# Group norm roots by token on 12 columns, spread back by a matmul, in the SSD mixer of a two-layer decoder step

## The reference, cut to what matters

```python
y = (y_diag + y_off) ...            # the scan over 4 chunks of 128 tokens, 4 heads a group
y = y + xs * d_skip[:, None]
y = y.reshape(b, l, D_INNER) * jax.nn.silu(z)
yg = y.astype(jnp.float32).reshape(b, l, SSD_GROUPS, D_INNER // SSD_GROUPS)
yg = yg * lax.rsqrt(jnp.mean(yg * yg, axis=-1, keepdims=True) + RMS_EPS)
y = (yg.reshape(b, l, D_INNER) * norm_g).astype(h.dtype)
return y @ w_out, new_conv, new_ssm
```

## Time and profile before

| what | value |
|---|---|
| median of 3 runs | 1629.84 us (1626.79 to 1630.45) |
| the profiled execution, its own time | 1631.33 us |
| the profiled execution, its span from first to last instruction | 1629.6 us |
| mean granted TensorE clock | 0.975 |
| busy: PE, DVE, ACT, POOL | 1523.5, 1179.9, 686.1, 596.4 us |
| the mixer's windows | from about 76 to 567 us of the span |

### The profile page before, as it was taken

One profiled execution on the slowest core, in us unless ns is written; L12 is line 12 of the kernel. 1 busy time (PEld: TensorE's weight loads), 2 busy tenths in 40 slices (PEclk: granted clock), 3 DMA queues, 4 the chain that ended last, 5 costly groups with the idle time before them and its releaser, 6 DMA issues.

```text
span 1629.6 us, 30561 instructions
## 1 busy us (share of the span) xinstructions
PE 1523.5 (93%) x12329; PEld 1501.4 (92%) x12329; DVE 1179.9 (72%) x1533; ACT 686.1 (42%) x1043; POOL 596.4 (37%) x573
## 2 busy tenths in 40 slices
PE   5898987989888799999999999999999999999996
PEld 5888877979888789999999999999999999999996
DVE  4678898883888788979798453464454897979943
ACT  4746645623566243434343333342233343434321
POOL 3076676650776732314156122200002141404801
PEclk9998998999999899999999999999999999999998
DMA  6444445443434332332323332223222323242311
GB/s 165 112 137 141 133 137 152 138 134 117 144 121 134 113 105 78 104 104 79 110 98 104 96 113 78 84 74 94 89 78 78 104 79 104 79 130 79 128 55 53
DMA packets 158931, 173.44 MB, mean 106 GB/s; under 512 B 13912, under 2 KB 146896, under 8 KB 158784
## 3 DMA queue, kind: packets, MB, share of 16 engines
q1 hardware_dynamic: 137032, 131.30, 25.6%
q0 software_dynamic: 9472, 26.50, 5.1%
q10 hardware_dynamic: 12288, 13.71, 3.0%
HBM read 159.53 MB, written 12.21 MB: 105 GB/s over the span
## 4 chain that ended last, share of the span: by engine, by line
PE 62%; DVE 1%; issue 1%; ACT 1%; POOL 0%; ACTq 0%; DVEq 0%
PE ps L941 28%; PE ps L662 17%; PE ps L966 15%; PE ps L1048 1%; PE ps L682 1%; DVE rstd L1806 0%; PE ps L1016 0%; DVE w_lo L2111 0%; PE ps L919 0%; PE ps L705 0%; PE ps L770 0%; POOL ssum L1595 0%; ACT arena L1539 0%; ACT w_hi L1434 0%; PE ps L1088 0%
## 5 line engine op out<-in xcount | busy, mean ns | idle before, releaser
L662 PE MATMUL ps<-h_hi,w_hi 128*128 128x260 f32 (+2 forms) x1296 | 276.8, 296 | 9.3 <-issue 4.7
L662 PE MATMUL ps<-h_lo,w_hi 128*128 128x260 f32 (+2 forms) x1296 | 266.8, 288 | 0.0
L662 PE MATMUL ps<-h_hi,w_lo 128*128 128x260 f32 (+2 forms) x1296 | 266.6, 288 | 0.0
L1434 ACT ACTIVATE w_hi<-w 128x512 fp32r<-128x512 f32 x232 | 138.2, 626 | 241.6 <-PE ps L941 161.6
L662 PEld LDWEIGHTS ps<-h_hi,w_hi 128*128 128x128 f32 x1296 | 208.4, 195 | 11.4 <-issue 9.2
L941 PE MATMUL ps<-h_hi,w_hi 128*128 128x260 f32 x1024 | 206.6, 283 | 4.7 <-DVE work L2143 4.5
L2111 DVE TENSOR_TENSOR w_lo<-w,w_hi 128x512 fp32r<-128x512 f32 x232 | 189.6, 844 | 25.1 <-ACT w_hi L1434 24.6
L662 PEld LDWEIGHTS ps<-h_lo,w_hi 128*128 128x128 f32 x1296 | 207.0, 195 | 0.0
L941 PE MATMUL ps<-h_hi,w_lo 128*128 128x260 f32 x1024 | 206.4, 283 | 0.0
L662 PEld LDWEIGHTS ps<-h_hi,w_lo 128*128 128x128 f32 x1296 | 206.4, 194 | 0.0
L941 PE MATMUL ps<-h_lo,w_hi 128*128 128x260 f32 x1024 | 206.0, 283 | 0.0
(11 more groups left out here) (259 smaller groups left out, 3617.3 us busy)
## 6 DMA issues: line engine op xcount, KB each, us to landing
w<-in_mlp_w_up SPq DMA_DIRECT2D x32, 1024.0 KB, 5.4
w<-in_mlp_w_down SPq DMA_DIRECT2D x32, 1024.0 KB, 5.1
w<-in_ssd_w_in SPq DMA_DIRECT2D x16, 1024.0 KB, 6.7
w<-in_cm_w_in SPq DMA_DIRECT2D x16, 1024.0 KB, 5.4
w<-in_ssd_w_in SPq DMA_DIRECT2D x16, 512.0 KB, 5.7
arena<-in_state_ssm POOLq DMA_DIRECT2D x64, 128.0 KB, 3.4
arena<-scr_a ACTq DMA_DIRECT2D x16, 512.0 KB, 3.6
arena<-scr_bc POOLq DMA_DIRECT2D x32, 256.0 KB, 3.7
```

What stands on the lines that cost most here:

```text
L662: mm = pe.matmul(ps[:, 2 * slot + b, 0:tn], w[:, pair.w_slot, k, col:col + P], x[:, k, t0:t0 + tn], start=(k == 0 and n == 0), stop=(k == ...
L1434: nc.scalar.activation(blocks(w_hi)[:, (p.ring + n) % 8], src, ACT.Copy)\
```

## The change

POOL's `y_sum` is gone. PE sums the squares of both tiles itself, into bank 6: for each of the four chunks two matmuls with one column of ones leave the sums token by token on the partitions (4 columns), and two more leave the 8 samples' sums on all partitions (8 columns). ACT takes the root of these 12 columns into `r_y`, and DVE their reciprocal (`y_recip`). ACT then scales the 128x128 identity by each of the 4 columns (`y_diagonal`, into `sq`), PE multiplies that with ones (`spread`), which puts the 512 reciprocals on every partition of bank 7, and `y_norm` reads them there. It has four instructions in place of two.

The same change moves work in the windows. DVE takes `decayed(g, 1)` ahead of `decayed(g, 0)`. `y_norm` stands behind the next weight split and `evac_unit(nxt, 0)`, `y_diag(g, 0)` behind `evac_unit(nxt, 1)`, the `xdte` product ahead of the second weight split and of `conv(nxt, 1)`, and `conv(nxt, 2)` behind `states(g)`. PE's `spread` stands behind `gu(nxt, 0)`, its waits for `comb_done` ahead of `state_out` and the B and C transposes become waits for `combine`'s first instruction, and `raw_tr(nxt, 1)` goes behind `gu(nxt, 2)`. After window 7 `spread(7)` stands between `gu(8, 6)` and `gu(8, 7)`.

```diff
--- before.py
+++ after.py
@@ -268,6 +268,7 @@
         ssm_stage = carve(2, N)
         xdts = carve(2, NS)
         ysmp = carve(2, NS)
+        r_y = carve(NC + NS)
         at[0] = dt_at
         dt_v = carve(T, parts=HEADS)
...
@@ -741,7 +743,7 @@
                     pe.wait_ge(crow_done, 2)
                     pe.wait_ge(convf_ready, 2)
                     if due(g - 1):
-                        pe.wait_ge(yroot_done, g - 1)
+                        pe.wait_ge(ynorm_done, 2 * (g - 1))
                 pe.transpose(ps[0:35, 7, t * P:(t + 1) * P], raw[:, t % 2, TP:TP + 35], ident[:, :])\
                   .then_inc(cst_tr, 1)
@@ -763,20 +765,32 @@
                 if g < 0:
                     return
-                pe.wait_ge(ysum_done, g + 1)
+                pe.wait_ge(ysq_done, 2 * g + 2)
+                pe.wait_ge(comb_done, 2 * g + 2)
+                parts = (ssum[:, :], sq[:, 0, :])
+                for c in range(NC):
+                    for i, part in enumerate(parts):
+                        pe.matmul(ps[:, 6, c:c + 1], part[:, c * CH:(c + 1) * CH], ones[:, 0:1], start=(i == 0), stop=(i == 1))
+                for i, part in enumerate(parts):
+                    mm = pe.matmul(ps[:, 6, NC:NC + NS], ones[:, 0:1].to_broadcast([P, P]), part[:, TP:T],
+                                   start=(i == 0), stop=(i == 1))
+                mm.then_inc(rms_done, 1)
+
+            def spread(g):
+
+                if g < 0:
+                    return
                 pe.wait_ge(cst_evac, min(g + 2, GROUPS))
-                pe.wait_ge(comb_done, 2 * g + 2)
-                for b in range(2):
-                    mm = pe.matmul(ps[:, 6 + b, 0:TH], ones[:, 0:1].to_broadcast([P, P]),
-                                   ssum[:, b * TH:(b + 1) * TH], start=True, stop=True)
-                mm.then_inc(rms_done, 1)
+                pe.wait_ge(diag_done, g + 1)
+                pe.matmul(ps[:, 7, :], ones[:, 0:1].to_broadcast([P, P]), sq[:, 0, 0:TP], start=True, stop=True)\
+                  .then_inc(spread_done, 1)
             def state_out(g):
                 if g < 0:
                     return
                 pe.wait_ge(hstep_done, 4 * g + 4)
-                pe.wait_ge(comb_done, 2 * g + 1)
+                pe.wait_ge(cchain, 6 * g + 1)
                 for i in range(2):
                     mm = pe.transpose(ps[:, 5, 256 + i * N:256 + (i + 1) * N], hprev[:, 3, i * P:(i + 1) * P], ident[:, :])
                 mm.then_inc(h4_tr, 1)
@@ -796,8 +810,8 @@
                                    A[:, 1, c * CH:(c + 1) * CH], start=True, stop=True)
                 mm.then_inc(cb_done, 1)
-                if due(2 * g - 1):
-                    pe.wait_ge(comb_done, 2 * g - 1)
+                if due(g):
+                    pe.wait_ge(cchain, 6 * (g - 1) + 1)
                 state_out(g - 1)
                 for i in range(2):
                     mm = pe.transpose(ps[0:NS, 5, i * N:(i + 1) * N], A[:, i, S0:CONV_N:TAPS], ident[:, :])
@@ -818,11 +832,12 @@
                 rms(g - 1)
                 if nxt < GROUPS:
                     gu(nxt, 0)
+                    spread(g - 1)
                 for i in range(2):
                     pe.wait_ge(xdt_done, 2 * g + i + 1)
                     for hh in range(2):
-                        pe.wait_ge(m_done, 4 * g + 2 * i + hh + 1)
+                        pe.wait_ge(m_done, 4 * g + 2 * (1 - i) + hh + 1)
                         for c in range(NC):
                             mm = pe.matmul(ps[hh * HD:(hh + 1) * HD, 4 + i, c * CH:(c + 1) * CH],
                                            xdt[:, c, (2 * i + hh) * HD:(2 * i + hh + 1) * HD],
@@ -835,13 +850,14 @@
                             mm = pe.transpose(ps[:, 6, c * P:(c + 1) * P], A[:, 0, c * CH:(c + 1) * CH], ident[:, :])
                         mm.then_inc(Btr_done, 1)
                         if nxt == GROUPS:
+                            spread(g - 1)
                             gu(nxt, 0)
                         gu(nxt, 1)
                         if nxt < GROUPS:
                             raw_tr(nxt, 0)
+                gu(nxt, 2)
                 if nxt < GROUPS:
                     raw_tr(nxt, 1)
-                gu(nxt, 2)
                 pe.wait_ge(xdte_done, g + 1)
                 pe.wait_ge(Btok_done, g + 1)
@@ -904,6 +920,7 @@
             rms(7)
             state_out(7)
             gu(GROUPS, 6)
+            spread(7)
             gu(GROUPS, 7)
             for m in range(KT):
                 tail_unit(m)
@@ -1225,9 +1242,8 @@
                 for i, dst in ((0, ssum[:, :]), (1, sq[:, 0, :])):
                     act_e.wait_ge(comb_done, 2 * g + i + 1)
                     if due(g):
-                        act_e.wait_ge(ysum_done, g)
-                    if due(2 * g):
-                        act_e.wait_ge(ynorm_done, 2 * g)
+                        act_e.wait_ge(rms_done, g)
+                        act_e.wait_ge(spread_done, g)
                     act_e.wait_ge(r_ready, 1)
                     nc.scalar.activation(dst, work[:, i, :], ACT.Square).then_inc(ysq_done, 1)
@@ -1236,8 +1252,21 @@
                 if g < 0:
                     return
                 act_e.wait_ge(rms_done, g + 1)
-                nc.scalar.activation(halves(ssum[:, :]), ps[:, 6:8, 0:TH], ACT.Sqrt, bias=eps[:, 0:1], scale=1.0 / 256)\
+                if due(g):
+                    act_e.wait_ge(ynorm_done, 2 * g)
+                nc.scalar.activation(r_y[:, :], ps[:, 6, 0:NC + NS], ACT.Sqrt, bias=eps[:, 0:1], scale=1.0 / 256)\
                   .then_inc(yroot_done, 1)
+
+            def y_diagonal(g):
+
+                if g < 0:
+                    return
+                act_e.wait_ge(yr_done, g + 1)
+                act_e.wait_ge(ident_ready, 4)
+                act_e.wait_ge(rms_done, g + 1)
+                for c in range(NC):
+                    ins = nc.scalar.activation(sq[:, 0, c * CH:(c + 1) * CH], ident[:, :], ACT.Copy, scale=r_y[:, c:c + 1])
+                ins.then_inc(diag_done, 1)
             def y_high(g):
@@ -1320,6 +1349,7 @@
                 if more:
                     fill(nxt, 0)
                     fill(nxt, 1)
+                y_diagonal(g - 1)
                 split_w(Pair(group_pair(nxt, 1) if more else J_OUT1 + 1))
                 y_high(g - 1)
                 if more:
@@ -1399,6 +1429,7 @@
             y_squares(7)
             split_w(Pair(J_TAIL))
             y_root(7)
+            y_diagonal(7)
             y_high(7)
             state_evac(7)
@@ -1588,12 +1619,6 @@
             nc.gpsimd.memset(dt_small[:, :], 0.0).then_inc(const_ready, 1)
             nc.gpsimd.memset(raw[:, :, 0:TAPS - 1], 0.0).then_inc(raw_zeroed, 1)
-            def y_sum(g):
-                if g < 0:
-                    return
-                pool.wait_ge(ysq_done, 2 * g + 2)
-                nc.gpsimd.tensor_tensor(ssum[:, :], ssum[:, :], sq[:, 0, :], ALU.add).then_inc(ysum_done, 1)
-
             def y_low(g):
                 if g < 0:
...
@@ -1867,17 +1890,25 @@
                                                    scalar=convf[:, k, tap:tap + 1], in1=act[:, g % 2, t, :],
                                                    op0=ALU.mult, op1=ALU.add).then_inc(tap_done, 1)
-            def y_norm(g):
+            def y_recip(g):
                 if g < 0:
                     return
                 dve.wait_ge(yroot_done, g + 1)
-                nc.vector.reciprocal(ssum[:, :], ssum[:, :]).then_inc(yr_done, 1)
+                nc.vector.reciprocal(r_y[:, :], r_y[:, :]).then_inc(yr_done, 1)
+
+            def y_norm(g):
+
+                if g < 0:
+                    return
                 dve.wait_ge(yr_done, g + 1)
+                dve.wait_ge(spread_done, g + 1)
                 for i in range(2):
-                    nc.vector.scalar_tensor_tensor(out=work[:, i, :], in0=work[:, i, :],
-                                                   scalar=feat[:, G_SSD + 2 * g + i:G_SSD + 2 * g + i + 1],
-                                                   in1=ssum[:, :], op0=ALU.mult, op1=ALU.mult).then_inc(ynorm_done, 1)
+                    gain = feat[:, G_SSD + 2 * g + i:G_SSD + 2 * g + i + 1]
+                    nc.vector.scalar_tensor_tensor(out=work[:, i, TP:T], in0=work[:, i, TP:T], scalar=gain,
+                                                   in1=r_y[:, NC:NC + NS], op0=ALU.mult, op1=ALU.mult)
+                    nc.vector.scalar_tensor_tensor(out=work[:, i, 0:TP], in0=work[:, i, 0:TP], scalar=gain,
+                                                   in1=ps[:, 7, :], op0=ALU.mult, op1=ALU.mult).then_inc(ynorm_done, 1)
             def y_low(g):
@@ -1995,36 +2026,38 @@
                         ps[:, 4 + i, :].rearrange("p (c h d) -> p c h d", c=NC, d=HD),
                         tokS[:, 0, :, 4 * g + 2 * i:4 * g + 2 * i + 2].unsqueeze(3).broadcast_to([P, NC, 2, HD]),
                         ALU.mult).then_inc(xdt_done, 1)
+                decayed(g, 1)
```

(20 more changed lines are left out.)

7 lines of the change are left out of this document (3 added, 4 removed).

## The result

| | before | after |
|---|---|---|
| median of 5 runs | 1627.98 us (1626.79 to 1630.45) | 1635.85 us (1634.15 to 1636.24) |
| profiled execution, its own time and span | 1631.33, 1629.6 | 1636.24, 1634.5 |
| mean granted clock | 0.975 | 0.972 |

The ratio after to before is 1.0045, with a 95% interval from 1.0031 to 1.0060. The change makes the kernel slower by 7 to 8 us, where 9.8 us less had been forecast. The two profiled spans are only 4.9 us apart: the profiled execution of before took 1631.33 us, more than any of the five behind its median, and that of after 1636.24, 0.4 above its own. The 4.9 is what the two traces can account for.

A forecast was written before the change was run, and what follows sets the result against it. DVE and POOL together bound the window, POOL's end as floor. Savings of 4.2 (windows 1 to 4, 6), 0 (window 5), 2.1 (window 0), 0.5 (window 7) and 3.0 (behind it), 9.8 in all, take 1629.84 to 1620.0 us; range 1608 to 1633.

The forecast's parts named there:

- The other side: Rival, chance 0.11: POOL's tail stays whole behind a late `y_low`, windows of 58.7 us, 1634 us in all.
- the gate: Point in the window where `y_high` is done and POOL may start `y_low`: 21.0 us after `combine`, before 19.0.
- The new chain ahead of `y_norm`: Mixer window: root, table load, Silu, scaled copies, `w_hi`, split, evacuation, half of `y_norm`, `y_high`; ends at 21.0 us.
- POOL's end is the floor: Mixer window: bound by DVE and POOL together; a faster DVE would wait at `sample(2, 3)` for POOL's last tile.
- I take 1.5 off (0 to 3): POOL's last three tiles, 29.0 us in window 2, shrink by 1.5 through less stretching of POOL's instructions.
- Window 4's gain reaches the end: Output product behind window 4: needs DVE's evacuations behind `combine(4)`, so that window's 0.85 us gain counts.
- Window 5 ... I put 0: Window 5 starts from PE, later against its root, so no gain is counted there: 0 us.
- the reordering ... brings at least that: Window 0, without `y_norm`: DVE comes 2.1 us after POOL; the new order gains 2.1, stopping at POOL's end.
- Behind window 7: End chain: `y_sum` 2.07 goes, `rms` 0.95 less, PE's clock 0.9, `spread(7)` costs 0.9; together 3.0 us less.
- The waits at `raw_tr`: Mixer: PE's 18.8 us of waits for DVE's evacuation mostly go, in exchange for its new wait ahead of `spread`.
- PE now stands still for up to 2.5 us: Mixer window: PE waits for the scaled copies ahead of `spread`, from 12.3 to 14.8 us; costed at nothing.
- turns into a wait of DVE for ACT: Mixer window: DVE's saved 3.2 us becomes idle time before `w_hi`, 5 us; the norm comes 2 us later for POOL.

The follow-up runs named there:

- norm_early: The changed kernel with `y_norm` moved ahead of the weight split, right behind `y_recip`; 1632.02 us, 1.0002 of before.
- whi_first: The changed kernel with ACT's `w_hi` right behind the root, ahead of the scaled copies and the z Silu; 1626.12 us, 0.9984 of before.
- low_on_dve: The changed kernel with `y_low` of windows 1 to 6 on DVE behind `conv(nxt, 0)` in place of POOL; 1622.73 us, 0.9965 of before.
- norm_only: The kernel before with the new norm in the old order, `y_norm` behind `evac_unit(nxt, 0)`; 1644.37 us, 1.0073 of before.
- order_only: The kernel before with the new order of the windows and the old norm; 1627.4 us, 0.9970 of before.
- whi_out: whi_first with the output product's first split and two evacuations ahead of `sample(4, 3)` and `combine(4)`; 1618.09 us, 0.9926 of before.
- whi_out_low: whi_out with `y_low` of windows 1 to 6 on DVE too; 1609.93 us, 0.9877 of before.
- out_ahead: The changed kernel with the output product's first split and two evacuations ahead of `sample(4, 3)` and `combine(4)`; 1627.16 us, 0.9973 of before.
- out_only: The kernel before with the output product's first split and two evacuations ahead of `sample(4, 3)` and `combine(4)`; 1625.83 us, 0.9985 of before.
- recip_short: The kernel before with the norm's reciprocal on 12 of 520 columns, output not normalized rightly; 1625.72 us beside 1630.0, 0.9973.

## Why the prediction was wrong

The outcome is that of the rival called "The other side", which had 0.11: the gate at 21, POOL's tail whole. It did not come by the means named for it, and that its 1634 lies so near to the 1635.85 is chance: `y_low` took 2.6, not 3.8, and the periods are 57.8, not its 58.7, while the gains that it took as sure in window 0 and at the end, 4.4 us, were 1.6.

- **The new chain ahead of `y_norm`**: right to a few tenths at each step, the 5 us of DVE's idle time included. norm_early and whi_first show that moving this gate forward gives back 0.4 to 0.6 of the norm's 0.7%.
- **"POOL's end is the floor"**: right for this kernel. low_on_dve shows it, and shows its limit: with POOL early enough, its tail waits for DVE and is 30.9 to 33.5 us long.
- **"I take 1.5 off (0 to 3)"** of POOL's three tiles: this is the step that failed in the windows. From the timelines, for the last three tiles in windows 1 to 4 and 6, the means per window:

| part of the tail, us | before | after |
|---|---|---|
| its 15 instructions | 15.07 | 14.02 |
| waits for the landing of the states, n = 2 and n = 3 | 2.66 + 2.92 | 3.56 + 2.76 |
| DMA issues and the gaps around them | 8.72 | 8.62 |
| start of n = 1 to end of n = 3 | 29.37 | 28.96 |

 The instructions did lose 1.05 us of their stretching, not far from the 1.5. But 0.74 of it came back as a longer wait for the states' transfer, mostly that of n = 2. Half of the tail is no computing at all, and I had read the stretched half as if the other would stay. In norm_only, order_only, whi_out and whi_out_low the tail of these windows is 28.4 to 30.3 us, and once 31.0. With 28.96 in place of 27.5, t = 24.0 and the 4.9 of the tail of DVE the period is 57.8, which is what it measured. Five windows: 6.9 us off. Why the transfer of n = 2 lands 0.9 us later was not tried, but the traces show what it goes with. It shares the DMA engines with a weight load that SP issues just behind it. What the weight queue moved while this state load of window 2 was under way (217.5 to 221.1 before, 218.6 to 223.4 after; packets, MB, share of 16 engines), before and then after:

```profile
q1 hardware_dynamic: 86, 0.09, 10.4%
```

```profile
q1 hardware_dynamic: 390, 0.40, 28.4%
```

 SP issues that weight load at t = 32.9 in both. POOL issues its state load at 31.4 before and, behind the late gate, at 32.5 after. In the five windows the two issues lie 1.5 to 3.1 us apart before, and 0.5 to 0.9 after. order_only also has them 0.5 to 0.9 apart, there because the weight load comes earlier, and waits 3.41 in the mean. norm_only has them 1.5 to 1.9 apart, and waits 2.67 to 2.89 in four windows of five.
- **"Window 4's gain reaches the end", "Window 5 ... I put 0"**: the second failure, 4.3 us. Window 4 had no gain to pass on. In the product I followed `combine(4)` alone and not when PE would arrive. PE came 4.2 us earlier, and the lower clock behind its wait costs 2.7 us. out_ahead and out_only fit this: the move takes away 6.6 us of wait and these 2.7, together 9.3 of the 9.5 measured. The other 1.6 us are window 5, which has the late gate like the other windows; with the gate mended in whi_first the stretch is 55.9 in place of 57.9.
- **"the reordering ... brings at least that"** in window 0: wrong by 1.8. POOL itself ended later, at 123.51 and not 121.71. Its tile n = 1 starts 3.7 us later, and 1.9 of it is made good in the tail. All four `decayed` products (3.87 us on DVE) and the split now run beside POOL's tile n = 0, and its four instructions on the outer products take 5.18 us together in place of 2.81, one of them, beside the split,

```profile
89.82 2.54 POOL L1683 TENSOR_TENSOR arena<-arena 128x256 f32<-128x256 f32 x1
```

 In order_only, which has the old norm, this product takes 2.69: it belongs to the order.
- **Behind window 7**: forecast 3.0 less, measured 1.3. `y_sum`'s 2.07 went. The small products did not give 0.95:

```profile
573.84 1.95 PE ps L773 x16
575.78 0.45 PE ps L775 x4
...
576.51 5.84 PE ps L664 x36
582.35 0.86 PE ps L785 x2
583.21 4.33 PE ps L664 x36
```

 The ten products (twenty records) take 2.40 us, 0.24 each, against the 2.10 of the wide ones, where I had put 1.15. I had let them overlap by half; one starts every 0.22 us. And that though the granted clock was 1.00 there, and 0.50 before. In the windows, where the clock was 1.00 in both, the forecast has no term for them at all: 2.15 us against 0.69. Windows of the stretch, after and then before:

```profile
573.80:576.30 2.50, 2.46 (x23) 2.46 (x23) 2.50 (x4) 2.48 (x2) 0.00 (x0) 1.00 0.12 36
576.50:582.30 5.80, 5.80 (x38) 5.80 (x37) 1.83 (x2) 1.93 (x6) 0.00 (x0) 0.71 0.99 312
```

```profile
569.80:571.90 2.10, 2.10 (x6) 1.61 (x7) 2.10 (x1) 0.88 (x1) 0.00 (x0) 0.50 0.92 266
```

 PE's wait fell from 2.9 to 1.7 us only, not by 2.9. The 1.5 us that a kept clock might give did not come either: the clock falls in the unit behind (0.71), and the two units take 5.84 + 4.33 where the same 72 records took 10.15 before. `spread` took 0.86; I had put 0.9.
- **The waits at `raw_tr`** The earlier trace rows went, as said. What PE saved there it waits ahead of `state_out`, 34.1 us in six waits (7.5 before). "In exchange" was right, and it was no gain. "PE now stands still for up to 2.5 us" was wrong: PE was busy until t = 16.0, and the one wait for the scaled copies in the windows is 1.1 us.
- **The saved DVE time "turns into a wait of DVE for ACT"**: right, and recip_short shows it was nearly worthless before too. The forecast used this for the gate and did not let it lower the chance of a gain.

The Trainium skill, in "GPSIMD Engine Reference", section "8. Key points", has the collision of GpSimd with DVE instructions that have two SBUF inputs. The runs agree: `y_low` took 2.6 beside products that read PSUM, and 4.4 to 4.7 beside the split in four windows of norm_early. Which of the two engines pays differs: the end of `y_low` at 209.90 lies beside `conv(nxt, 0)`, whose three DVE instructions from 208.78 took 4.23 us, where those from 218.92 took 2.42. The drain of 1.38 us behind a table load, which the Trainium skill gives in "ScalarE: Activation LUTs", section "What ACT_TABLE_LOAD costs", does not show: the load at 197.61 takes 1.28, and the Silu starts at 198.91.

Still open: whether the state load comes earlier once the weight load is moved away from it, which only the traces say; what PE's narrow products and the lower clock behind them cost; and why single windows differ by a microsecond between kernels that are alike there. norm_early and low_on_dve were not run together.

## What to carry to other kernels

- Before costing a chain that is to be shortened on an engine, ask what that engine would wait for next if the work were gone. Here it was `w_hi`: 25 us of reciprocal was worth 4. A run with the cheap form in its old place tells it in one step.
- The engine that closes a stage is not helped by relief of another, unless work is handed over. In POOL's tail fifteen instructions and the transfers between them share the time about evenly, and what the instructions lost here (1.05 us) the landings took back for the most part (0.74). Count the issues and landings as a part of their own, and look at what other transfer is issued next to each.
- Where a stage ends in a wait of PE, look at both ends of the wait. An earlier arrival with the same release makes it longer, and the price can be a lower clock behind it (7.5 us of wait and 2.7 more in the unit behind it, against 2.3 and none). Then put what PE waits for ahead of the stage's closing chain.

## What the runs showed of the hardware

- PE's clock behind a wait: 2.28 us left it at 1.00; after 7.52 us it was 0.50, the 1.2 GHz level, from 363.1 to 368.9, with matmul pairs at 0.64, and 0.95 from 368.9 to 372. After 4.79 us in order_only it was 0.50 for 4 us as well. The length of the wait alone does not tell it: in norm_only PE waited 2.09 us at the same place, and the clock was 0.50 from 368.6 to 372.0.
- PE's clock without a wait: behind the ten narrow products (2.15 us at 1.00, PE busy throughout) it was 0.77 over the unit in five of six windows, and that unit took 7.4 us in place of 6.05.
- `y_low`'s two halves of 520 columns: 2.59 us together in the change, 4.4 to 4.7 beside DVE's split of 2048 columns. A 128x256 product on POOL: 0.61 at its least, 2.54 beside DVE's split.
- Products of a single column are not cheap by their width: the ten of `rms` took 2.40 us at a granted clock of 1.00, the two of 260 columns before 2.10 at 0.50.
- A state load that POOL issues itself: 1.42 us for issuing it, and 2.6 to 4.1 until POOL may use it. The second load landed 3.1 to 3.5 us behind its issue where other queues moved under 0.1 MB meanwhile (windows 1 to 4 and 6 before), and 3.6 to 4.8 where they moved about 0.25 to 0.45 MB (the same windows after).
